# Input projection, gates and SSD in one stage, and the modulation's second part in the mLSTM stage

## The reference

```python
mod = silu(c) @ w_ada + b_ada                 # six groups of 1024: sh1, sc1, g1, sh2, sc2, g2
h = rmsnorm(x, norm1_g) * (1 + sc1) + sh1
proj = h @ w_in
q, k, v, o, ig, fg, z, xbc, dt = split(proj)  # 6,688 columns
q, k = causal_conv_silu([q, k])               # four taps
h_a = scan(mlstm_chunk, (q, k, v, ig, fg))    # 8 heads, chunks of 128 tokens
h_a = head_layernorm(h_a) * sigmoid(o)
x, B, C = causal_conv_silu(xbc)
y_b = scan(ssd_chunk, (x, dt, B, C)) + d_skip * x   # 16 heads, 2 groups of B and C
y_b = rmsnorm(y_b * silu(z), ssm_norm_g)
x = x + g1 * ([h_a, y_b] @ w_out)
h2 = rmsnorm(x, norm2_g) * (1 + sc2) + sh2
x = x + g2 * peer_ffn(h2)                     # product-key retrieval of experts
```

## Time and profile before

| | us |
|---|---|
| median of 3 runs (2706.91 to 2710.17) | 2708.55 |
| profiled execution | 2709.52 |
| its span | 2707.5 |
| input projection (85.0 to 399.9) | 314.9 |
| gates (399.9 to 432.0) | 32.1 |
| convolutions of the samples (432.0 to 446.7) | 14.7 |
| mLSTM (446.7 to 541.9) | 95.2 |
| SSD with modulation (541.9 to 687.7) | 145.8 |

### The profile page before, as it was taken

One profiled execution on the slowest core, in us unless ns is written; L12 is line 12 of the kernel. 1 busy time (PEld: TensorE's weight loads), 2 busy tenths in 40 slices (PEclk: granted clock), 3 DMA queues, 4 the chain that ended last, 5 costly groups with the idle time before them and its releaser, 6 DMA issues. The chain is left out here.

```text
span 2707.5 us, 34419 instructions
## 1 busy us (share of the span) xinstructions
PE 2373.6 (88%) x12991; PEld 2024.1 (75%) x12991; DVE 1533.9 (57%) x2618; ACT 808.2 (30%) x1054; POOL 1022.2 (38%) x465
## 2 busy tenths in 40 slices
PE   5799985488629859999999998999999999999996
PEld 3699984355527759877887787888888888888885
DVE  2599006755650021578878987777555555555541
ACT  1322333211010021333333444445433232322222
POOL 0244440000310023365566567545655444444430
PEclk8899996766559979999999999999999999999998
DMA  4232310044543025555554678757665555554430
GB/s 165 78 94 92 95 47 6 8 125 117 155 113 100 21 64 126 139 140 140 140 140 117 170 216 257 214 159 221 194 241 205 201 198 186 197 190 186 186 124 32
DMA packets 304574, 379.21 MB, mean 140 GB/s; under 512 B 14218, under 2 KB 257310, under 8 KB 300345
## 3 DMA queue, kind: packets, MB, share of 16 engines
q1 hardware_dynamic: 209364, 289.72, 35.3%
q10 hardware_dynamic: 91648, 75.50, 8.6%
q0 software_dynamic: 3456, 12.58, 1.5%
HBM read 294.66 MB, written 79.13 MB: 138 GB/s over the span
## 5 line engine op out<-in xcount | busy, mean ns | idle before, releaser
L1685 POOL TENSOR_TENSOR utL_hid<-ut_hid,utH_hid 128x1024 fp32r<-128x1024 f32 x128 | 348.7, 2724 | 323.4 <-ACT utH_hid L1681 322.8
L1695 PE MATMUL bank<-pH,utH_hid 128*128 128x512 f32 x1024 | 406.4, 397 | 13.5 <-POOL utL_hid L1685 13.5
L1695 PE MATMUL bank<-pH,utL_hid 128*128 128x512 f32 x1024 | 399.3, 390 | 0.0
L1695 PE MATMUL bank<-pL,utH_hid 128*128 128x512 f32 x1024 | 399.2, 390 | 0.0
L2179 PE MATMUL bank<-area,work 128*128 128x512 f32 x1536 | 350.8, 389 | 0.0
L2179 PEld LDWEIGHTS bank<-area,work 128*128 128x128 f32 x1536 | 288.4, 188 | 59.7
L482 PE MATMUL ps_in<-hH_in,wH_in 128*128 128x260 f32 x832 | 236.9, 285 | 13.0 <-POOL wL_in L466 12.1
L1674 DVE STREAM_TRANSPOSE ut_hid<-u_hid 128x1024 f32<-128x1024 f32 x128 | 158.8, 1241 | 144.0 <-POOL utL_hid L1685 124.8
L482 PE MATMUL ps_in<-hL_in,wH_in 128*128 128x260 f32 x832 | 235.8, 283 | 0.0
L482 PE MATMUL ps_in<-hH_in,wL_in 128*128 128x260 f32 x832 | 235.6, 283 | 0.0
L1695 PEld LDWEIGHTS bank<-pH,utH_hid 128*128 128x128 f32 x1024 | 192.8, 188 | 56.3 <-POOL utL_hid L1685 18.7
(11 more groups left out here) (445 smaller groups left out, 4339.3 us busy)
## 6 DMA issues: line engine op xcount, KB each, us to landing
u_hid<-in_peer_u_dram SPq DMA_DIRECT2D x256, 256.0 KB, 5.2
work<-in_peer_v_dram SPq DMA_DIRECT2D x64, 1024.0 KB, 5.0
hidden_dram<-ge_hid ACTq DMA_DIRECT2D x64, 512.0 KB
gates_dram<-area ACTq DMA_DIRECT2D x16, 2048.0 KB, 10.7
wb_in<-in_w_in_dram SPq DMA_DIRECT2D x26, 1024.0 KB, 5.3
wm_ssd<-in_w_ada_dram SPq DMA_DIRECT2D x32, 512.0 KB, 3.9
area<-hidden_dram SPq DMA_DIRECT2D x16, 1024.0 KB, 6.8
area<-gates_dram SPq DMA_DIRECT2D x16, 1024.0 KB, 8.8
```

Source lines behind the costliest of these rows:

```text
L1685: self.nc.gpsimd.tensor_tensor(self.utL[:, u % 2], self.ut[:, u % 2], self.utH[:, u % 2].bitcast(F32), ALU.subtract).then_inc(self.low, 1)
L1695: mm = self.nc.tensor.matmul(self.pa[u % 2][:, :], w[:, u % 2, k, :], x[:, k, :], start=(n == 0), stop=(n == 3 * KD - 1))
```

## The change

`input_phase`, `gates_phase` and `ssd_phase` go; `front_phase` takes their place, with the classes `Gates` and `Ssd`, whose methods give each engine its part. The chunks are unrolled and in another order: v (8), x, B and C (12), z (8), o (8), q and k (16). The gates' parts stand between the first chunks: ScalarE's behind chunks 0, 1, 5 and 6, VectorE's ahead of chunk 0 and behind 1, 2, 3, 4, 6 and 10, TensorE's behind chunk 9. SSD works in four sub-rounds of 4 heads. Each has eight steps k = 0 to 7, and each step stands behind half a chunk of products (24 matmuls), in chunks 20 to 35; two last steps stand in chunk 36. Steps 0 and 1 turn the result of the sub-round before and transpose x; steps 2 to 5 spread a head's `cum` and make one chunk's state product; steps 4 to 7 make the heads' products; step 7 turns the state. Ahead of the first of them TensorE waits for all twelve convolutions of x, B and C and for the gates. VectorE's convolutions read the taps where they lie, so the two small copies go. `pick` is now 64 by 16 and is broadcast by its access pattern. The tiles of gates and SSD lie in parts of `proj` that are not filled yet, and the gates' results in the place of x, which is therefore written to DRAM in the split stage (2.1 MB) and loaded back at the end of the output projection. The 32 modulations move to `mlstm_phase` with four weight buffers and two of `mrows`: 16 in the head loop (behind the second and fourth chunk of each head), 10 behind the loop, 6 in the final turns. There one bank `mb` for the spread maxima replaces two.

```diff
-def input_phase(nc, A, S, XH, XL):
...
-def gates_phase(nc, A, S, R, O):
...
-def ssd_phase(nc, A, S, R, O):
...
+class Ssd:
+    HG = 4
+    SUBS = H_B // HG
...
+    def tensor(self, pe, s, k):
+        nc, S, m, HG = self.nc, self.S, self.m, self.HG
+        tok, g = self.tok, s // 2
+        if k < 2 and s:
+            f = 2 * (s - 1) + k
+            if k == 0:
+                pe.wait_ge(m["so_ready"], s)
+                pe.wait_ge(m["y_out"], HG * s)
+                pe.wait_ge(m["inter_out"], NC * s)
+            else:
+                pe.wait_ge(m["t_out"], f)
+            for c in range(NC):
+                mm = nc.tensor.transpose(self.px[:, c * L:(c + 1) * L], self.Y[(s - 1) % 2][:, c, 2 * k:2 * k + 2, :].rearrange("p h d -> p (h d)"), S.ident[:, :])
+            mm.then_inc(m["t_in"], 1)
...
+        if 2 <= k < 6:
+            h, c = k - 2, k - 2
+            n = HG * s + h
+            if k >= 4:
+                self.weighted(pe, s, h - 2)
+            if h == 0:
+                pe.wait_ge(m["bc_out"], g + 1)
+            if n:
+                pe.wait_ge(m["xs"], n)
+            nc.tensor.matmul(self.cb[:, :], S.pick[:, n:n + 1].to_broadcast((SPLIT, P)), self.R.split_cum[:, :], start=True, stop=True).then_inc(m["spread"], 1)
+            i = NC * s + c
+            if c == 0:
+                pe.wait_ge(m["x_out"], 2 * s + 2)
+            if i:
+                pe.wait_ge(m["state"], i)
+                pe.wait_ge(m["inter_out"], i)
+            if c:
+                nc.tensor.matmul(self.a[:, 256:512], tok(NX + 10 + g, c), self.ST.rearrange("p h d -> p (h d)"), start=True, stop=True)
+            nc.tensor.matmul(self.a[:, 0:256], self.Bt[:, c, :], self.xw[:, c].rearrange("p h d -> p (h d)"), start=True, stop=True).then_inc(m["inter_in"], 1)
+        if k >= 6:
+            self.weighted(pe, s, k - 4)
...
+    def weighted(self, pe, s, h):
+        nc, m = self.nc, self.m
+        n = self.HG * s + h
+        pe.wait_ge(m["weighed"], n + 1)
+        if n >= 2:
+            pe.wait_ge(m["y_out"], n - 1)
+        for c in range(NC):
+            mm = nc.tensor.matmul(self.py[:, (n % 2) * 256 + c * P_B:(n % 2) * 256 + (c + 1) * P_B], self.E[n % 2][:, c, :], self.xdt[:, c, h, :], start=True, stop=True)
+        mm.then_inc(m["y_in"], 1)
...
+    def step(self, dve, own, s, c, Y):
+        S, m, V, HG = self.S, self.m, self.nc.vector, self.HG
+        hs = slice(HG * s, HG * s + HG)
...
+        own(V.tensor_tensor(self.ST, self.ST, bcast(S.bb[:, hs, c], 2, P_B), ALU.mult))
+        V.tensor_tensor(self.ST, self.ST, pu, ALU.add).then_inc(m["state"], 1)
+        own(V.tensor_tensor(self.tmp, pi, bcast(S.cols[:, c, 7, hs], 2, P_B), ALU.mult))
+        if c > 2:
+            dve.wait_ge(m["y_out"], HG * s + c - 2)
+        V.tensor_tensor(Y[:, c], Y[:, c], self.tmp, ALU.add).then_inc(m["inter_out"], 1)
...
+def front_phase(nc, A, S, R, O, XH, XL):
...
+    chunks = [(2 * D + c * P, NV + c, "copy", c) for c in range(8)]
+    chunks += [(Z0 + D + c * P, NX + c, "conv", (16 + c, V_CBW + c, 12, V_CBB + c)) for c in range(12)]
+    first_z = len(chunks)
+    chunks += [(Z0 + c * P, NZ + c, ACT.Silu, c) for c in range(8)]
+    chunks += [(3 * D + c * P, NO + c, ACT.Sigmoid, c) for c in range(8)]
+    chunks += [(c * P, NQ + c, "conv", (c, V_CAW + c, 16, V_CAB + c)) for c in range(16)]
...
+    hooks = {2 * (first_z + 4 * s) + k: (s, k) for s in range(Ssd.SUBS) for k in range(8)}
+    hooks[2 * (first_z + 16)], hooks[2 * (first_z + 16) + 1] = (Ssd.SUBS, 0), (Ssd.SUBS, 1)
...
+            for n, (_, slot, kind, _) in enumerate(chunks):
+                if n + 2 < len(chunks):
+                    move_high(n + 2)
+                if kind == "conv":
+                    act.wait_ge(convd, convs(n) + 1)
+                    nc.scalar.activation(S.proj[:, slot, 0:T], y[:, convs(n) % 2, :], ACT.Silu).then_inc(used, 1)
+                elif on_act[n]:
+                    act.wait_ge(product, n + 1)
+                    nc.scalar.activation(split(slot), ps[n % 2][:, :, 0:HN], kind).then_inc(by_act, 1)
+                for part, at in enumerate((0, 1, 5, 6)):
+                    if n == at:
+                        G.scalar(act, own, part)
+                for hook in (2 * n + 1, 2 * n + 2):
+                    if hook in hooks and hooks[hook][0] < Ssd.SUBS:
+                        X.scalar(act, *hooks[hook])
...
+        @block.tensor
+        def _(pe):
+            for n in range(len(chunks)):
+                pe.wait_ge(low, n + 1)
+                if n >= 2:
+                    pe.wait_ge(by_act if on_act[n - 2] else by_dve, before(n - 1, on_act[n - 2]))
+                for h in range(2):
+                    tok = slice(h * HN, (h + 1) * HN)
+                    for k in range(KD):
+                        for p, (a, b) in enumerate(((wH, XH), (wH, XL), (wL, XH))):
+                            mm = nc.tensor.matmul(ps[n % 2][:, h, 0:HN], a[n % 2][:, k, :], b[:, k, tok],
+                                                  start=(k == 0 and p == 0), stop=(k == KD - 1 and p == 2))
+                    if h == 1:
+                        mm.then_inc(product, 1)
+                    if 2 * n + h in hooks:
+                        if 2 * n + h == 2 * first_z:
+                            pe.wait_ge(used, 12)
+                            pe.wait_ge(G.spread, 2)
+                        X.tensor(pe, *hooks[2 * n + h])
+                if n == 9:
+                    G.tensor(pe, 0)
...
+            def mod_turn(c):
+                pe.wait_ge(mrows_out, c + 1)
+                M.turn(pm[:, 9 * c:9 * c + 9], mrows[c % 2]).then_inc(mturned, 1)
+            def modulation(c):
+                if c:
+                    mod_turn(c - 1)
+                else:
+                    pe.wait_ge(cleared, 1)
+                pe.wait_ge(wm_in[c % AHEAD], 16 * (c // AHEAD + 1))
+                M.multiply(row_bank, wm[c % AHEAD]).then_inc(m_product, 1)
...
                     step(h, c)
                     if h + 2 < H_A:
                         prepare(h + 2, c)
+                    if c % 2:
+                        modulation(2 * h + c // 2)
...
+            for c in range(16, 26):
+                modulation(c)
             pe.wait_ge(normed, 1)
             for h in range(H_A):
                 if h >= 2:
                     pe.wait_ge(hmoved, h - 1)
                 for c in range(NC):
                     mm = nc.tensor.transpose(qk[h % 2][:, c * L:(c + 1) * L], num[:, c, h, 0:P], S.ident[:, :])
                 mm.then_inc(hturned, 1)
+                if h < 6:
+                    modulation(26 + h)
+            mod_turn(MODS - 1)
...
                 nc.scalar.activation(sq[:, :, :], num[:, c, :, 0:P], ACT.Square).then_inc(squared, 1)
+                modulation(16 + 2 * c)
+                modulation(17 + 2 * c)
+            modulation(24)
+            modulation(25)
             act.wait_ge(var_ready, NC + 1)
             own = Chain(act, act_own)
             own(nc.scalar.activation(var[:, :, :], var[:, :, :], ACT.Ln))
             nc.scalar.activation(var[:, :, :], var[:, :, :], ACT.Exp, scale=-0.5).then_inc(rooted, 1)
+            for c in range(26, MODS):
+                modulation(c)
...
+            if spill is not None:
+                sp.dma_start(spill, S.xT.rearrange("p k n -> p (k n)")).then_inc(rows_out, 16)
+                sp.wait_ge(rows_out, 16)
...
+            sp.dma_start(*reload).then_inc(reloaded, 16)
+            sp.wait_ge(reloaded, 16)
```

More of the change, by code:

```diff
@@ L663, in _, with tensor @@
+    def tensor(self, pe, part):
+        nc, S, R = self.nc, self.S, self.R
+        if part == 0:
+            pe.wait_ge(self.acted, 2)
+            for q, r in enumerate((R.a, self.row["inter"], self.row["w"], self.row["em"], R.cum, R.dt, self.rw, self.re)):
                 n = H_A if q < 4 else H_B
```

827 lines of the change are left out of this document (376 added, 451 removed).

## The result

The changed kernel takes 2620.99 us (median of 4 runs, 2619.68 to 2622.98) against 2708.53 before: a ratio of 0.9677, 95% interval 0.9661 to 0.9694. That is 87.5 us less, and the forecast was 72.5. The profiled execution takes 2619.89, its span is 2618.0.

What follows compares the result with a forecast made beforehand. Limits were read by stage: projection by TensorE, gates a chain, mLSTM mixed, SSD 80% TensorE-busy at 0.62 clock. Removing 177.9 us and returning 104.9 gave -73.0, from 2709.5 to 2636.5 profiled, 2636 median; range 2602 to 2683.

Steps and rivals of the forecast that it cites:

- late eviction: Early merged stage: chunk 2's eviction, behind VectorE's first gates part, holds chunk 4; +1.5 us (0.5 to 2.5).
- first SSD step: Merged stage: TensorE waits for the twelfth x, B, C convolution, and the clock may fall once; +6.5 us (3 to 15).
- SSD matmuls: Merged stage: SSD's matmuls among the products run at full clock, with possible float32 switch costs; +49 us (44 to 54).
- VectorE's answers: SSD steps: VectorE answers late, its SBUF-to-SBUF operations stretched by GpSimd's subtraction in odd steps; +16 us (4 to 30).
- mLSTM: head loop: mLSTM head loop: sixteen modulations in a nearly full TensorE loop, delaying keys and values; +13 us (7 to 20).
- mLSTM: logarithm: mLSTM normalisation: ScalarE's last four modulation copies stand ahead of the logarithm the final scaling needs; +6 us (2 to 9).
- mLSTM: final turns: mLSTM final turns: six modulations at a 2.25 us period, 16.3 us instead of 8.2; +8 us (7 to 9).
- spill: Split stage: waits at its end for x's 2 MB write to DRAM; +1 us (0 to 5), reload 0.
- The first rival: Merged stage: clock falls at stalled steps and next products pay; +32 us at 16 steps, 2668; chance 0.14.
- the second: Rival: clock stays low through the whole interleaved part; +124.5 us, 2760; chance of slower 0.07.
- ScalarE's table loads: z and o chunks: two loads each, 1.28 us apiece, no added cost taken; with the skill's drain 4 us, 2640.
- everything below is what comes back: Opening of the sum: gates and SSD stages go, 177.9 us removed; the terms listed after are all that returns.

Runs made afterwards that it cites:

- the fused update: Changed kernel with the state's update as four operations taking state times decay plus the PSUM product at once, replacing one multiply and one add; 2609.0 us, ratio 0.9635.
- the kernel with all four edits: Changed kernel with state update fused, two v chunks moved behind x/B/C, no modulation copies between last Square and logarithm, GpSimd's first sample-stage multiply behind VectorE's small preparations; 2596.5 us.

## Why the prediction was right, and where it was wrong

The direction, the mechanism and the range held; the median was 15 us lower than forecast. In the profiled executions 9.6 of the difference belong to a stage that the prediction left out and 5.3 to the mLSTM, which at 116.9 also lies under the 118 to 126 of the forecast. The merged stage, forecast at 392 us, took 391.7. The terms in the profiled executions, predicted and measured (the measured ones sum to -90.1, the spans differ by 89.5):

```
removed: gates and SSD stages            177.9    177.9
products of the convolution chunks        -2.8     -3.3   (5.87 to 5.75 a chunk)
gates in the stream                       +3       +3.2
late eviction                             +1.5     +1.4
first SSD step                            +6.5     +6.2   (two v chunks late)
SSD matmuls                              +49      +51.6   (71.2 without steps, less 6.2 and 13.4)
VectorE's answers                        +16      +13.4   (11.5 by the fused update, 1.9 waited at L722)
last convolution                          +3.7     +4.0
mLSTM: head loop                         +13      +11.0
mLSTM: logarithm                          +6       +5.9
mLSTM: final turns                        +8       +4.8
spill                                     +1       -0.8
samples                                    0       -9.6
```

**The SSD matmuls at full clock.** Right: 51.6 against 49, inside its bounds of 44 to 54. The one price that no row had shown, the switch between float32 steps and products, stayed small: at the most 51.6 - 44 = 7.6 us for 34 steps. The 51.6 is a remainder, but the kernel with all four edits gives nearly the same directly: by its timeline 147.1 us lie between the last product ahead of the steps and the first behind them, 94.4 of them for 33 half chunks and 1.9 for waits, so 50.8.

**VectorE's answers.** The mechanism was right to the operation: state times decay in the odd steps, prolonged to the end of GpSimd's subtraction. The forecast had TensorE wait for the state and the collected y; by the view it waits for the weighed scores, which stand behind the state's update in VectorE's queue, and for the weighed x. Of the waits foreseen ahead of steps 2, 4, 5 and 6 (counted from 0), those of 2 (0.6), 4 (1.4) and 6 (0.8 to 1.1) are there; step 5 did not wait. So 13.4, the clock included, instead of 16.

**The clock.** The first rival gave it 32 us, the second 124. It fell three times, at the first step and twice behind a late step 4, and cost some 2 us for the two (11.5 less 9.4 of waits); the window of the interleaved part shows 0.96, and 1.00 without the waits. The row of 490 to 500 in the earlier trace rows, in which TensorE's gaps are of 0.3 to 0.9 us, had pointed the right way. The Trainium skill ("TensorE: Matmul & The Clock Gate", "A second HAM failure mode: psum-queue depth-cycling") tells of a clock that swings when TensorE idles briefly between groups of matmuls. The trace agrees in part: of twelve waits in the steps, nine of 0.8 us and more, three pulled the clock down.

**ScalarE's table loads.** In the changed kernel the next instruction again starts 0.01 us behind a load of 1.28, the load itself 0.02 behind the instruction ahead of it (585.69 to 585.71), and no wait of TensorE leads to ScalarE's exponentials. By the row nothing was added, and nothing came. The drain that the Trainium skill adds ("ScalarE: Activation LUTs", "What ACT_TABLE_LOAD costs") would have shown there; no run here shows it.

**The mLSTM.** Head loop and logarithm were right to 2 us. The final turns were over by 3: the price of 2.25 us per turn was taken from a row at the lower clock, and the clock rose after the third turn, so the later ones took 1.34:

```profile
595.74 1.11 PE L1144 MATMUL qk_ml<-ident,num_ml 128*128 128x128 f32 x4
...
597.98 1.12 PE L1144 MATMUL qk_ml<-ident,num_ml 128*128 128x128 f32 x4
...
601.30 0.66 PE L1144 MATMUL qk_ml<-ident,num_ml 128*128 128x128 f32 x4
...
602.64 0.66 PE L1144 MATMUL qk_ml<-ident,num_ml 128*128 128x128 f32 x4
```

The loads of the modulation's weights were no term, as said, but not for the reason given: with two buffers TensorE waited 9.2 us for them in the SSD stage (the row of L548 above); with four, its waits in the mLSTM stage have none for a DMA.

**What was left out.** The step that failed is "everything below is what comes back": it let the sum end with the stages that the change touches. A stage behind them kept its code and lost 9.6 us, since two engines start there within a microsecond of each other and the one that is first decides. Its size was to be had: the same effect was priced in the earlier trace rows and used for the SSD steps, and the sample stage of the kernel before showed operations on 64 columns at 1.8 us. Which way it would go was not, since some 1.6 us of alignment decided it (GpSimd 0.26 us ahead of VectorE before, 1.4 behind it after). The lower end of the range, 2602, was also worked out for a profiled execution; by the prediction's own step to the median it is 2601.

**A right sum that hid a wrong reading.** Taking the SSD stage away as a whole was right. But it would have misled on its parts: the modulations' 42.5 us of busy time and 9.2 us of waits in that stage were worth 20 us, which the mLSTM stage took back.

## What to carry to other kernels

Work of TensorE that stalls by itself on another engine's answers, and so runs at the lower clock, can be cut into steps of 0.4 to 2.5 us between long runs of products: here it cost 71 us instead of 126, because the products filled the waits and held the clock. The price is then set by the answers that come later than one run of products, so look for operations of VectorE from SBUF to SBUF that meet GpSimd, those with two SBUF inputs above all, and give them an input in PSUM or another place. And when two stages meet such a race by a few tenths of a microsecond, order it by a wait: otherwise a change ahead of it can move the time by 9 us, and is praised or blamed for it.

## What had not been expected of the hardware

An operation of VectorE on 64 columns takes 0.28 us ahead of a GpSimd multiply and 1.78 behind its start; a row of them beside a row of GpSimd's multiplies takes turns with these, nearly one for one, so eleven small operations cost some 15 us. Operations of 64 columns with one input in PSUM took 277 ns on average in the same place where one of 256 columns from SBUF took 1378 on average. And of four idle gaps of 1.4 us between half chunks of products two pulled the clock down and two did not; seven of 0.6 to 1.1 us did not either, and the one of 4.1 at the first step did.
